# A hybrid diffusion layer: two instead of three ordinary column pairs in the first feed-forward, its token sums built between the modulation rounds, and one buffer for the late modulation weights

## The reference

```python
D_MODEL = 1024; SEQ = 128; DEC_SEQ = 512; D_FF = 2816; N_MOD = 9

def swiglu(h, w_in, w_out):
    g, u = jnp.split(h @ w_in, 2, axis=-1)
    return (jax.nn.silu(g) * u) @ w_out

def trunk_layer(x, cond, w_mod, b_mod, norm_pre, norm_post, ffn_w_in, ffn_w_out, ...):
    mod = (jax.nn.silu(cond) @ w_mod + b_mod)[:, None, :]
    sh1, sc1, g1, sh2, sc2, g2, sh3, sc3, g3 = jnp.split(mod, N_MOD, axis=-1)
    h = rms_norm(x, norm_pre[0]) * (1.0 + sc1) + sh1
    x = x + 0.5 * g1 * rms_norm(swiglu(h, ffn_w_in[0], ffn_w_out[0]), norm_post[0])
    h = rms_norm(x, norm_pre[1]) * (1.0 + sc2) + sh2
    m, s_f, s_b = mixer(h, w_in, w_four, hgrn_gain, w_hgrn, w_out, lb, s0_f, s0_b, rows)
    x = x + g2 * rms_norm(m, norm_post[1])
    h = rms_norm(x, norm_pre[2]) * (1.0 + sc3) + sh3
    x = x + 0.5 * g3 * rms_norm(swiglu(h, ffn_w_in[1], ffn_w_out[1]), norm_post[2])
    return x, s_f, s_b
```

## Time and profile before

| | |
|---|---|
| median of 3 runs | 1399.71 us (1398.91 to 1399.75) |
| the profiled execution | 1400.03 us, its span 1398.2 us |
| TensorE busy | 1377.5 us, 99% of the span |
| VectorE / ScalarE / GpSimd busy | 54% / 42% / 52% |
| mean granted TensorE clock | 0.998 |

### The profile page before, as it was taken

One profiled execution on the slowest core, in us unless ns is written; L12 is line 12 of the kernel. 1 busy time (PEld: TensorE's weight loads), 2 busy tenths in 40 slices (PEclk: granted clock), 3 DMA queues, 4 the chain that ended last, 5 costly groups with the idle time before them and its releaser, 6 DMA issues.

```text
span 1398.2 us, 23518 instructions
## 1 busy us (share of the span) xinstructions
PE 1377.5 (99%) x9547; PEld 1259.3 (90%) x9547; DVE 749.4 (54%) x1117; ACT 583.4 (42%) x948; POOL 724.2 (52%) x530
## 2 busy tenths in 40 slices
PE   6999999999999999999999999999999999999998
PEld 5889898999788888999999999989999999998886
DVE  4686565766712431478776312135977666665033
ACT  5243333434524663244445222257343443355243
POOL 1475545465865672323223433542576555677653
PEclk9999999999999999999999999999999999999999
DMA  9856666232545651212112222333123223335465
GB/s 324 281 169 212 218 231 211 61 92 91 168 131 167 194 174 49 61 54 62 52 41 66 76 76 75 104 108 91 46 76 88 79 77 91 91 106 156 131 196 180
DMA packets 219455, 173.34 MB, mean 124 GB/s; under 512 B 6537, under 2 KB 183893, under 8 KB 219221
## 3 DMA queue, kind: packets, MB, share of 16 engines
q1 hardware_dynamic: 216608, 170.61, 39.4%
q10 hardware_dynamic: 2740, 1.24, 0.3%
HBM read 168.65 MB, written 3.17 MB: 123 GB/s over the span
## 4 chain that ended last, share of the span: by engine, by line
PE 91%; DVE 3%; POOL 2%; SPq 1%; DMA 1%; ACT 1%; issue 0%; DVEq 0%; ACTq 0%
PE PP L822 32%; PE PP L620 23%; PE PP L639 9%; PE PP L641 9%; PE PP L640 9%; PE PP L678 2%; PE PP L893 2%; PE PP L664 1%; POOL T_lo L556 1%; PE PP L1030 1%; DMA W_in<-in_ffn_w_in 1%; PE PP L1046 1%; DVE BSUM L1932 0%; POOL W_lo L556 0%; PE PP L1100 0%
## 5 line engine op out<-in xcount | busy, mean ns | idle before, releaser
L547 POOL TENSOR_TENSOR W_lo<-W_in,W_hi 128x512 fp32r<-128x512 f32 (+1 forms) x304 | 379.3, 1273 | 450.6 <-ACT W_hi L1238 446.3
L556 POOL TENSOR_TENSOR W_lo<-W_in,W_hi 128x512 fp32r<-128x512 f32 x112 | 176.2, 1586 | 182.5 <-ACT S_hi L1462 180.6
L1238 ACT ACTIVATE W_hi<-W_in 128x1024 fp32r<-128x1024 f32 x143 | 150.9, 1056 | 220.1 <-PE PP L641 116.6
L639 PE MATMUL PP<-W_hi,Mlo 128*128 128x512 f32 x440 | 172.1, 391 | 1.5 <-DVE Mhi L2007 1.1
L641 PE MATMUL PP<-W_hi,Mhi 128*128 128x512 f32 x440 | 171.3, 389 | 0.0
L640 PE MATMUL PP<-W_lo,Mlo 128*128 128x512 f32 x440 | 171.2, 389 | 0.0
L620 PE MATMUL PP<-Hhi,W_hi 128*128 128x320 f32 (+2 forms) x608 | 146.7, 316 | 0.0
L620 PE MATMUL PP<-Hlo,W_hi 128*128 128x320 f32 (+2 forms) x608 | 142.3, 309 | 0.0
L620 PE MATMUL PP<-Hhi,W_lo 128*128 128x320 f32 (+2 forms) x608 | 142.2, 309 | 0.0
L822 PE MATMUL PP<-Hhi,W_hi 128*128 128x320 f32 x452 | 141.3, 313 | 0.9 <-POOL W_lo L556 0.5
L822 PE MATMUL PP<-Hhi,W_lo 128*128 128x320 f32 x452 | 139.6, 309 | 0.0
(11 more groups left out here) (298 smaller groups left out, 3010.0 us busy)
## 6 DMA issues: line engine op xcount, KB each, us to landing
W_in<-in_ffn_w_out SPq DMA_DIRECT2D x176, 256.0 KB, 3.2
W_in<-in_ffn_w_in SPq DMA_DIRECT2D x84, 512.0 KB, 4.5
modl<-in_w_mod SPq DMA_DIRECT2D x14, 2048.0 KB, 8.1
W_in<-in_w_in SPq DMA_DIRECT2D x32, 512.0 KB, 3.8
modw<-in_w_mod SPq DMA_DIRECT2D x8, 1024.0 KB, 12.0
HL<-g_rows SPq DMA_DIRECT2D x6, 512.0 KB, 5.8
V_in<-in_w_in SPq DMA_DIRECT2D x10, 256.0 KB, 4.0
O_in<-in_w_out SPq DMA_DIRECT2D x10, 256.0 KB, 5.4
```

Of the source, the lines that this page charges most:

```text
L547: return nc.gpsimd.tensor_tensor(lo[:, k0:k1, :], full[:, k0:k1, :], hi[:, k0:k1, :].bitcast(fp32), ALU.subtract)
L556: return nc.gpsimd.tensor_tensor(lo, full, hi.bitcast(fp32), ALU.subtract)
L639: mm(out, xh, wh, start=lead and kk == 0, stop=False)
L1238: A(W[i][0], W[i][2], ACT.Copy).then_inc(hi_done, 1)
```

## The change

The first feed-forward now has two ordinary pairs and 20 of the seven-product scheme (the second keeps 3 and 19). `EARLY_PAIRS` and `SEVEN` become tuples, indexed by the feed-forward. Late blocks follow slabs 2 and 3 and then each of the first 12 pairs; all of them go through one buffer, each load waiting for the product of the block before. `keep_busy` before the second round has 14 transposes instead of 24. `fold_mod` of the second round stands after one part of a slab instead of two, and `early_mod(2)` one feature tile earlier. The token sums of the first feed-forward are built in pieces: two after the second round, T1 and half of T2 after the third, and the rest after the fourth. The low halves of T1 and T2 go from GpSimd to VectorE.

```diff
-EARLY_PAIRS = 3
-SEVEN = FT - EARLY_PAIRS
+EARLY = (2, 3)
+SEVEN = tuple(FT - e for e in EARLY)
+SEVEN_AT = (0, SEVEN[0])
+SEVEN_END = (SEVEN[0], SEVEN[0] + SEVEN[1])
+HIDDEN = (EARLY[0], EARLY[0] + EARLY[1], EARLY[0] + 2 * EARLY[1])
...
-    ("in0", 2 * EARLY_PAIRS, [0, 1, 2, 11, 0, 1], False),
-    ("in0s", 2 * SEVEN, [12, 2, 0, 1], False),
+    ("in0", 2 * EARLY[0], [0, 1, 2, 11], False),
+    ("in0s", 2 * SEVEN[0], [8, 9] + [12, 2, 0, 1] * SEVEN[0], False),
...
-MOD_AFTER = [2, 3, 5]
+MOD_AFTER = [2, 3]
...
         def load_mod(i):
-            s = int(i == 1)
-            sp.dma_start(modl[s][:, :, :], wm[:, :, (MOD_EARLY + i) * 512:(MOD_EARLY + i + 1) * 512])\
-                .then_inc(sem(f"modl_in{s}"), 16)
+            if i:
+                sp.wait_ge(sem("mod_mm"), MOD_EARLY + i)
+            sp.dma_start(modl[:, :, :], wm[:, :, (MOD_EARLY + i) * 512:(MOD_EARLY + i + 1) * 512])\
+                .then_inc(sem("modl_in"), 16)
...
         load_mod(0)
-        sp.wait_ge(sem("mod_mm"), MOD_EARLY)
+        sp.wait_ge(sem("h0_32"), KT)
+        load_pair(BASE["in0s"], w0, EARLY[0])
+        load_pair(BASE["in0s"] + 2, w0, EARLY[0] + 1)
         load_mod(1)
...
+        load_pair(BASE["in0s"] + 4, w0, EARLY[0] + 2)
+        load_mod(2)
+        load_mod(3)
...
         pe.wait_ge(sem("x0_feat"), NCH)
-        keep_busy(24, PP[2][:, 1, 0:P])
+        keep_busy(14, PP[2][:, 1, 0:P])
         early_mod(1)
...
         first_slab(0, (0,))
+        fold_mod(1, P, modrow[1])
         first_slab(1, (0,))
-        fold_mod(1, P, modrow[1])
         first_slab(0, (1,))
         first_slab(1, (1,))
         first_slab(2, (0, 1))
+        early_mod(2)
+        first_slab(0, (2,))
+        fold_mod(2, 2 * P, modrow[2])
+        for n in (1, 2):
+            first_slab(n, (2,))
         for n in range(3):
-            first_slab(n, (2,))
-        early_mod(2)
-        first_slab(0, (3,))
-        fold_mod(2, 2 * P, modrow[2])
-        first_slab(1, (3,))
-        first_slab(2, (3,))
+            first_slab(n, (3,))
...
                 if b != 1 and grp == 0:
-                    for j in range(EARLY_PAIRS + 2 * m + 3, min(FT, EARLY_PAIRS + 2 * m + 5)):
+                    e = EARLY[b // 2]
+                    for j in range(e + 2 * m + 3, min(FT, e + 2 * m + 5)):
                         whole_high(b // 2, j)
...
+        def b11_b12():
+
+            dve.wait_ge(sem("h0_ready"), KH)
+            whole(0, 0, BSUM[0])
+            link(whole(0, HALF, T3_IN[0]))
+
+        def t1_and_half_of_t2():
+
+            dve.wait_ge(sem("mod_mm"), 3)
+            V.tensor_tensor(T1[2][:, :, :], T3_IN[0][:, :, :], BSUM[0][:, :, :], ALU.subtract)\
+                .then_inc(sem("t_made"), 1)
...
+        def first_token_low(n, x, made):
+
+            dve.wait_ge(sem("t_made"), made)
+            dve.wait_ge(sem("t_hi"), n + 1)
+            hi, lo, full = x
+            V.tensor_tensor(lo[:, :, :], full[:, :, :], hi[:, :, :].bitcast(fp32), ALU.subtract)\
+                .then_inc(sem("t_lo"), 1)
...
+            if r == 1:
+                b11_b12()
+            if r == 2:
+                t1_and_half_of_t2()
+        rest_of_t2_and_t4()
...
-        for j in range(EARLY_PAIRS):
+        for j in range(EARLY[0]):
             dve.wait_ge(slab_done, 2 * j + 2)
             dve.wait_ge(sem("gate_ready"), j + 1)
             V.tensor_tensor(two(M32[:, j, :]), two(TT[0][:, :]), halves(1), ALU.mult).then_inc(sem("hid_ready"), 1)
             if j == 0:
-                token_combinations(0)
-            if j == 1:
+                first_token_low(0, T1, 2)
+                first_token_low(1, T2, 3)
                 first_sums(0, 0)
                 last_sum(0, 0)
                 lows(0, 0)
```

More of the change, by code:

```diff
@@ L374, in ring_entries @@
         entries = []
-        for _ in range(SEVEN):
+        for _ in range(max(SEVEN)):
             entries.append((RING[s1], RING[s2], RING[s4]))
@@ L585, in _ @@
                 continue
+            if i == BASE["out1A"]:
+                second_token_lows()
             if i in (BASE["out0A"], BASE["out1A"]):
-                token_lows(int(i == BASE["out1A"]))
-            if i in (BASE["out0A"], BASE["out1A"]):
-                for p in range(SEVEN):
+                for p in range(SEVEN[int(i == BASE["out1A"])]):
                     seven_low(int(i == BASE["out1A"]), p)
@@ L861, in seven_products @@
             if first:
-                pe.wait_ge(sem("t_lo"), 3 * f + 2)
-                pe.wait_ge(sem("hid_ready"), (1 + f) * EARLY_PAIRS)
+                pe.wait_ge(sem("t_lo"), 2 * f + 2)
+                pe.wait_ge(sem("hid_ready"), HIDDEN[f])
+            elif second and not f:
+                pe.wait_ge(sem("u3_done"), 1)
             elif not second:
@@ L927, in _ @@
         fold_mod(3, 3 * P, modrow[3])
-        first_slab(1, (4,))
-        first_slab(2, (4,))
+        for n in (1, 2):
+            first_slab(n, (4,))
         for k in range(5, KT):
@@ L933, in _ @@
         late_mods(2)
-        for j in range(1, EARLY_PAIRS):
+        for j in range(1, EARLY[0]):
             if j == 1:
@@ L949, in _ @@
         last_mod = MOD_LATE - len(MOD_AFTER) - 1
-        for p in range(SEVEN):
+        for p in range(SEVEN[0]):
             seven_products(0, p)
@@ L1196, in _ @@
         pe.wait_ge(sem("h_lo"), NCH + 3)
-        for j in range(EARLY_PAIRS):
+        for j in range(EARLY[1]):
             if j == 0:
@@ L1498, in seven_gates @@
                 else:
-                    for j in range(EARLY_PAIRS):
+                    for j in range(EARLY[f]):
                         whole_high(f, j)
@@ L1504, in seven_gates @@
                 A(x, x, ACT.Silu).then_inc(sem("gate_a"), 1)
-                if p + 2 >= SEVEN:
+                if p + 2 >= SEVEN[f]:
                     after_slab(i)
                     after_slab(i + 1)
-            second_gate(f, SEVEN - 1)
-            for j in range(EARLY_PAIRS, EARLY_PAIRS + 3):
+            second_gate(f, SEVEN[f] - 1)
+            for j in range(EARLY[f], EARLY[f] + 3):
                 whole_high(f, j)
-        for j in range(EARLY_PAIRS):
+        for j in range(EARLY[0]):
             after_slab(2 * j)
-            gate_out(j, (two(TT[0][:, :]), halves(2 if j == 1 else 0)))
-            if j == 1:
-                token_highs(0)
-            if j == 2:
+            if j == 0:
+                token_high(T1, 1)
+            gate_out(j, (two(TT[0][:, :]), halves(2 * j)))
+            if j == 0:
+                token_high(T2, 2)
+                token_high(T4, 3)
+            else:
                 gate_highs(0, 0)
@@ L1705, in _ @@
             c0, c1 = G_COLS[grp]
-            for j in range(EARLY_PAIRS):
-                n = (1 + grp) * EARLY_PAIRS + j
+            for j in range(EARLY[1]):
+                n = HIDDEN[grp] + j
                 after_slab(BASE[stage] + 2 * j)
@@ L2346, in _ @@
         early_hidden(0, 1)
-        token_combinations(1)
+        second_tokens()
         early_hidden(0, 2)
```

210 lines of the change are left out of this document (103 added, 107 removed).

## The result

| | before | after |
|---|---|---|
| median, first measurement | 1398.97 us | 1407.75 us (1403.74 to 1410.9, 7 runs), ratio 1.0058 [1.0042, 1.0075] |
| median, second measurement | 1399.09 us | 1405.52 us (1403.56 to 1407.2, 5 runs), ratio 1.0043 [1.0031, 1.0055] |
| profiled execution, its span | 1400.03, 1398.2 us | 1403.74, 1401.8 us |
| TensorE busy | 1377.5 us | 1374.4 us |

The forecast was 1403.5 us, at most 1406. The profiled execution took what the sum had given (1403.8 us), but it was the shortest of its seven runs. So two things have to be explained: the 3.7 us of this execution, and the 2 to 4 us by which the median lies above it. The kernel before has no such difference: its profiled execution lay within 1.1 us of its medians. *Granted clock* is the share of TensorE's full clock that it gets; a *fall* is a stretch in which that share is 0.50 while TensorE is at work.

What follows compares the result with a forecast made beforehand. TensorE, busy 99% of the span, was taken as the bound. Profiled 1400.03 us + 0.8 for the start + 3.0 for the out stage = 1403.8, for the median 1403.5 us; range 1399.5 to 1406 us.

Steps and rivals of the forecast that it cites:

- The rival on the clock: TensorE's clock falls behind the second fold's gap, dense work takes twice as long: +1.7 us, 1405.2 us; chance 0.13.
- Step 2: Ten fewer transposes (1.9 us) before round two's product, which awaits its load: begins at 26.3 instead of 27.20, 0.9 us gained.
- Step 3: Round two's earlier fold still waits for its row until 30.9; TensorE 0.9 us behind, first late product at 58.1.
- VectorE's new work there costs nothing by its own length: Token sums after rounds two and three: VectorE waited for the next fold anyway; uncovered, each sum would delay about 1.5 us.
- Step 4: Second late block's reload through one buffer takes 10.2 us, landing at 70.3; TensorE waits 2 to 3 us after slab 3.
- the ring rule: DMA engines take a ring's descriptors in order, so loads behind the late block take nothing from it: 8.0 us holds.
- Step 5: First pair by seven products takes 12.5 us, from 72.2 to 84.7; the start is 0.8 us slower in all.
- the lower bound: Late block's reload in 8.0 us: pair starts at 69.95, T3's low half holds it up to 0.9 us; -0.6.
- Step 6: Out stage: regrouped hidden tiles come late, 0.6 us at slab 2, slab 8 2.3 us later through slab 7; +3.0 us.
- the upper bound of step 4: Late block's reload takes 11.6 us, landing at 71.7, as if a second following load cost further; start +2.2.

Runs made afterwards that it cites:

- experiment 8: Kernel before the change with only the changed kernel's grouping of hidden tiles at the first feed-forward's out stage: 1402.88 us, ratio 1.0024.
- experiment 11: experiment 6's kernel with first gate's Silu ahead of T1's high half, T3's sum and first hidden tile ahead of T4's sum: 1400.41 us, ratio 1.0007.
- experiment 3: Changed kernel with filler transposes put into six gaps of TensorE, 24 of them ahead of round two's product: 1404.85 us, ratio 1.0037.
- experiment 10: Kernel before the change with 14 transposes instead of 24 ahead of the second round's product: 1400.33 us, ratio 1.0005.
- experiment 1: The changed kernel measured once more without any edit: 1405.52 us, ratio 1.0043; its profiled execution took 1407.2 us.
- experiment 2: Changed kernel with 24 transposes again instead of 14 ahead of the second round's product: 1406.64 us, ratio 1.0055.
- experiment 9: experiment 6's kernel with slab 2's high half moved behind the second round's modulation row on ScalarE: 1399.65 us, ratio 1.0.
- experiment 4: Changed kernel with one more hidden tile's high half ahead of the first feed-forward's out stage, undoing the shift of groups: 1402.17 us, ratio 1.0025.
- experiment 5: Changed kernel with the four small LB operations on VectorE moved from ahead of T3's low half to the sixth pair: 1404.07 us, ratio 1.0037.
- experiment 6: Changed kernel with both the LB operations in the sixth pair and one more hidden tile ahead of the out stage: 1400.62 us, ratio 1.0007.
- experiment 12: experiment 11's kernel with the second late block's load bringing only half of its columns (other half old data): 1400.01 us, ratio 1.0005.

## Why the prediction was wrong

The time was outside the range, on the slow side. The step that failed is the turn from the sum to the median: "Sum. 1400.03 + 0.8 + 3.0 = 1403.8, and for the median 1403.5 us". The rival on the clock had a chance of 0.13 and one stretch at 1.7 us. In its place the runs showed a median 2 to 4 us above the execution that the sum describes, with up to two falls of 1.7 us in an execution, and waits that vary with the landing of loads.

- **The sum hit the shortest execution, and by luck**: 1403.8 forecast, 1403.74 measured; start +0.8, out stage and the rest +2.8 against 3.0. Inside both halves terms were off and cancelled (below). The base wasn't clean either: the old kernel's execution had a fall at its first fold and this one of the changed kernel had none. At the first late product that was worth 0.3 us, by experiment 8 (56.89 without the fall, 57.23 with it).
- **The clock.** Its price was right (1.7 us for a stretch), its frequency wasn't. The prediction looked for one gap, that of the second fold. The changed kernel has four in which a fall was seen, in it or in a variant: the first fold (experiment 11), the second, the fourth product and slab 7. Two fell in one execution (3.4 us). That this makes up most of the medians' 2 to 4 us above the shortest execution is supported by one profiled run and by the mean clocks of twelve; the runs without a profile don't say where their clock fell. It isn't the whole: experiment 3's execution without a fall took 1406.31 us.
- **Step 2** had the product at 26.3; it came at 26.68, by the load. Its price of 1.9 us for ten transposes was read off a stretch at the lower clock; 24 take 2.82 us at full clock, ten 1.2, and there was no gain of 0.9 us to be had by leaving them out (experiments 8 and 10).
- **Step 3** took slab 2's load to land as before. It landed earlier (the fold is at 29.90, not 30.9), and the 0.9 us weren't lost: the first late product is at 57.09, not 58.1. That is this execution's load; in others of the same order slab 2 landed later, with the first late product at 57.65 (experiment 1) and 57.96 (experiment 2). That the fold waits for a row behind slab 2's high half on ScalarE was right; experiment 9 removed it.
- **"VectorE's new work there costs nothing by its own length"** in step 3 was wrong for its last piece. The rest of T2, T3 and T4 stands ahead of the first hidden tile, and T1's high half ahead of the first Silu; slab 3 waits 1.45 us. It costs little in the end, since the late block behind it isn't there sooner (experiment 11).
- **Step 4** had the reload at 10.2 us and a wait of 2 to 3; it took 9.3 us (issued at 59.07, there by 68.40; 8.6 to 9.4 in experiments 1 to 4) and the two waits together are 2.1 us. By the ring rule of the Trainium skill ("DMA: Bandwidth & Descriptors", "Queues, rings and completion order") it would have been the 8.0 us of a load with nothing behind it; 9.3 lies between both, and no run here loaded the block with no slab behind it to settle it.
- **Step 5** promised a first pair without waits, and named the four small operations only for the lower bound. They cost 1.65 us at a landing near the lower bound. This error cancelled those of steps 3 and 4, which is why 84.66 looks exact. The right total didn't come from right terms.
- **Step 6** had the mechanism right: experiment 8 puts the grouping alone at +3.2 us in the old kernel and experiment 4 its undoing at -3.3 us in the new one, falls of the clock included in both. Its arithmetic for slab 7 is exact in the old kernel: there slab 7 waits 3.02 us and begins 32.4 us after the stage's start (376.36 - 343.92), which is 376.6 in the old trace. In the changed kernel's execution tile 15 was at VectorE at 374.93, 1.0 us earlier against the stage than step 6 had it, as the `w_out` load came earlier. So slab 7 waits 1.81 us instead of over 3, and slab 8 begins 1.3 us later instead of nearly 3. The wait at slab 10 and the later steps, which step 6 didn't have, brought the total near 3.0.
- **The range** reached for the upper bound of step 4 plus one fallen stretch. It had no case with two.

By the ratios, the change's loss of 6 us (1.0043) divides into 2.5 us for the grouping of hidden tiles (to 1.0025; by the medians 3.3), 2.5 for the LB operations once the grouping is mended (to 1.0007; alone, in experiment 5, they gave only 0.8), and 1.0 for the fold's wait (to 1.0), which isn't shown. Each part carries 1 us and more of the intervals. Without these three losses, fewer ordinary pairs and the single late buffer come out even with the kernel before. No version tried here beats it by what a measurement can tell.

## What to carry to other kernels

When an order of work is shifted by one unit (a pair, a tile), look at every group whose size was tuned to it: here an index that moved by one put a tile two slabs nearer to its use, which was nearly half of the loss. Before a row's duration goes into a sum, look at the granted clock over it: the 4.49 us of 24 transposes were 2.82 at full clock. For each wait that a change adds on TensorE, add to the sum what a fall of the clock behind it would cost, with a chance for each, since the median is made of both kinds of execution and one profile shows only one. And before a stall is removed, look at what ends next at the same place: the fold's wait, slab 3's and the late block's each hid another of up to its own length.

## What the runs showed of the hardware

- After a wait of TensorE of much the same length the granted clock fell in one execution and not in another: behind 1.44 us at the second fold it fell (experiment 5), behind 1.24 us at the same place it didn't (experiment 6); at slab 7 it fell behind 2.32 us (experiment 1) and 3.02 (experiment 8), and not behind 1.81 (the changed kernel) or 2.34 (experiment 5). At the first fold it fell behind 1.37 us (the kernel before) and 1.64 (experiment 11), and not behind 1.11 (experiment 1). The length of the last gap alone doesn't decide it.
- One and the same load doesn't land at the same time in each execution. ScalarE's wait for slab 2's load ended at 28.30 us in the changed kernel, at 28.86 in experiment 1, which is the same program, and at 29.74 in experiment 3, and the second fold stands at 29.90, 30.46 and 31.34.
- A fallen stretch cost about 1.7 us of work in the executions of experiments 1, 4, 5, 8 and 11. In that of experiment 12 it lasted longer, behind a wait of 1.82 us at the second fold: 0.42 x 8.0 = 3.4 us, by the windows of 30 to 38 us and of what follows:

```profile
30.00:38.00 8.00, 7.08 (x29) 0.58 1.10 348
38.00:60.00 22.00, 22.00 (x159) 1.00 0.66 203
```
